# Pooling and attention gates of a decoder layer's merge: four of eight K pairs by seven products instead of eight

## The reference

```python
g_pool, g_attn, g_ret = split(sigmoid(u @ w_gate), 3)      # w_gate: 2048 x 6144
merged = g_pool * (pool_out @ w_pool_out) + g_attn * (attn_out @ w_attn_out) \
       + g_ret * (ret_out @ w_ret_out)                     # K = 1024, 1024, 2048
return merged @ w_out
```

## Time and profile before

| | us |
|---|---|
| median of 3 runs (2372.71 to 2373.50) | 2372.98 |
| the profiled execution | 2372.41 |
| its span, first to last instruction | 2370.6 |
| TensorE busy | 2356.8 (99%) |
| VectorE busy | 1750.5 (74%) |
| ScalarE busy | 1243.2 (52%) |

### The profile page before, as it was taken

How to read it: one execution, slowest core, us unless ns; L and a number is a source line. 1 busy time by engine, 2 the same in 40 slices (tenths; PEclk the granted TensorE clock), 3 DMA queues, 4 the chain that set the end, 5 groups by cost and what they waited for, 6 DMA issues and landing times. The chain is left out here.

```text
span 2370.6 us, 33710 instructions
## 1 busy us (share of the span) xinstructions
PE 2356.8 (99%) x10613; PEld 1945.0 (82%) x10613; DVE 1750.5 (74%) x2057; ACT 1243.2 (52%) x1490; POOL 205.9 (9%) x398
## 2 busy tenths in 40 slices
PE   9999999999999999999999999999999999999998
PEld 7888888888888888888888888888888888888887
DVE  6999999978876555655545545555799999997886
ACT  6555555555545454444544444444655555555553
POOL 1212112110000000000000000000021211211000
PEclk9999999999999999999999999999999999999999
DMA  7766666665675555565656566655666666666665
GB/s 236 220 212 203 216 219 222 212 221 191 209 240 172 163 175 178 159 188 157 204 187 196 190 198 193 189 185 194 207 213 227 206 218 207 221 212 214 204 204 195
DMA packets 266605, 477.44 MB, mean 201 GB/s; under 512 B 21152, under 2 KB 54608, under 8 KB 265392
## 3 DMA queue, kind: packets, MB, share of 16 engines
q1 hardware_dynamic: 252752, 453.04, 59.6%
q0 software_dynamic: 13616, 23.53, 3.0%
q10 hardware_dynamic: 176, 0.07, 0.0%
HBM read 460.84 MB, written 4.19 MB: 196 GB/s over the span
## 5 line engine op out<-in xcount | busy, mean ns | idle before, releaser
L1260 ACT ACTIVATE w_hi<-w_raw 128x1024 fp32r<-128x1024 f32 (+1 forms) x848 | 863.6, 1021 | 985.9 <-PE acc L781 732.1
L1641 DVE TENSOR_TENSOR w_lo<-w_raw,w_hi 128x1024 fp32r<-128x1024 f32 (+1 forms) x848 | 991.8, 1172 | 507.5 <-ACT w_hi L1260 503.0
L779 PE MATMUL acc<-w_hi,xT_hi 128*128 128x512 f32 x1552 | 609.2, 393 | 1.0 <-DVE w_lo L1641 1.0
L781 PE MATMUL acc<-w_hi,xT_lo 128*128 128x512 f32 x1552 | 604.4, 389 | 0.0
L780 PE MATMUL acc<-w_lo,xT_hi 128*128 128x512 f32 x1552 | 604.1, 389 | 0.0
L779 PEld LDWEIGHTS acc<-w_hi,xT_hi 128*128 128x128 f32 x1552 | 291.4, 188 | 63.0 <-issue 2.5
L781 PEld LDWEIGHTS acc<-w_hi,xT_lo 128*128 128x128 f32 x1552 | 291.3, 188 | 61.1
L780 PEld LDWEIGHTS acc<-w_lo,xT_hi 128*128 128x128 f32 x1552 | 291.5, 188 | 59.3
L696 POOL DMA_DIRECT2D act_raw<-blocks x352 | 174.9, 497 | 736.4 <-DVE blocks L1978 647.5
L779 PE MATMUL acc<-w_hi,act_hi 128*128 128x512 f32 x560 | 218.2, 390 | 0.1
L780 PE MATMUL acc<-w_lo,act_hi 128*128 128x512 f32 x560 | 217.9, 389 | 0.0
(11 more groups left out here) (269 smaller groups left out, 2601.4 us busy)
## 6 DMA issues: line engine op xcount, KB each, us to landing
w_raw<-in_ffn_up_dram SPq DMA_DIRECT2D x352, 512.0 KB, 4.2
w_raw<-in_ffn_down_dram SPq DMA_DIRECT2D x176, 512.0 KB, 4.2
w_raw<-in_w_gate_dram SPq DMA_DIRECT2D x96, 512.0 KB, 3.8
w_raw<-in_w_in_dram SPq DMA_DIRECT2D x72, 512.0 KB, 3.6
w_raw<-in_w_in_dram SPq DMA_DIRECT2D x128, 256.0 KB, 2.9
w_raw<-in_w_ret_out_dram SPq DMA_DIRECT2D x32, 512.0 KB, 3.7
w_raw<-in_w_out_dram SPq DMA_DIRECT2D x32, 512.0 KB, 4.2
act_raw<-blocks POOLq DMA_DIRECT2D x352, 32.0 KB, 3.8
```

What stands on the lines that cost most here:

```text
L779: pe.matmul(pair[m][:, :], xh, wh, start=(first and kk == 0), stop=False)
L781: mm = pe.matmul(pair[m][:, :], xl, wh, start=False, stop=(last and kk == KG - 1))
L1260: act.activation(w_hi[:, s, cols], w_raw[:, s, cols], ACT.Copy).then_inc(w_rounded, 1)
L1641: dve.tensor_tensor(w_lo[:, s, cols], w_raw[:, s, cols], w_hi[:, s, cols].bitcast(f32), ALU.subtract).then_inc(w_split, 1)
```

## The change

- The merge's order of strips becomes: retention gate (groups 0 to 7), retention branch (8 to 15), pool gate and attention gate together (16 to 31), pool branch (32 to 35), attention branch (36 to 39).
- In the joint stretch, K pairs 4 to 7 of both gates are quads at groups (17, 18), (21, 22), (24, 25), (28, 29); K pairs 0 to 3 are plain. `merge_products` does the seven products with four extra banks; VectorE makes the weight sums, VectorE and ScalarE split them, and VectorE combines the banks into `gate_sb` and `hid_sb`, on which ScalarE then does the sigmoids.
- The weight sums use `dt_raw`, `dt_hi`, `dt_lo`. So h is stored to the output tensor behind the first block's residual (`h_away(0)`) and loaded again behind the last quad of the merge (`h_again`); the load of `post_gain` moves from the last head to the same place, ahead of it.
- Once, in pass 0: the ratio of the norm factors is spread over the columns by one matmul of ones with a diagonal (behind group 1), VectorE scales tile 1 with it and makes the token sums at steps 2 to 8.

Left out of the diff below: the allocation of semaphores, the quad counters, the token sums (one product and four sums of 128 x 512 and 128 x 1024), and `h_parked` and `h_back` counts.

```diff
+MERGE_QUADS = ((17, 18, 4), (21, 22, 5), (24, 25, 6), (28, 29, 7))
+MERGE_GATE0 = {16: 0, 19: 1, 20: 2, 23: 3}
+MERGE_GATE1 = {26: 0, 27: 1, 30: 2, 31: 3}
+NMQ = len(MERGE_QUADS)
+M_KT = KG * MERGE_QUADS[0][2]
+M_TILES = KG * NMQ
+M_JOINT, M_POOL, M_ATT = 2 * GD, 4 * GD, 4 * GD + GH
+NM = 4 * GD + 2 * GH
...
+        MQ_A = {ng: j for j, (ng, nu, k) in enumerate(MERGE_QUADS)}
+        MQ_B = {nu: j for j, (ng, nu, k) in enumerate(MERGE_QUADS)}
+        MT_AT = {ng - 3 + pair: (j, pair) for j, (ng, nu, k) in enumerate(MERGE_QUADS) for pair in range(2)}
...
+                for n in range(NM):
+                    for quads in (MQ_A, MQ_B):
+                        if n - SLOTS in quads:
+                            sp.wait_ge(t_summed, 3 * (merge_quad(c, quads[n - SLOTS]) + 1))
+                            sp.sem_inc(slot_summed, 1)
+                    w, col = source[n]
+                    cols = w[:, :, ds(c * STRIP + col, STRIP)]
+                    if n == GD:
+                        sp.wait_ge(w_split, group("merge", c, n) + 1)
+                        sp.sem_inc(slot_split, 1)
+                        sp.dma_start(slot(n % SLOTS), cols).then_inc(w_landed[n % SLOTS], 16)
+                    else:
+                        load("merge", c, n, cols)
...
+            def h_away(blk):
+                for m in range(MT):
+                    wait_h(pool, blk, m, CH - 1)
+                    pool.dma_start(out[0][m * P:(m + 1) * P, :], h[:, m, :]).then_inc(h_parked, 16)
+            def h_again(last_quad, src):
+                pool.wait_ge(t_used, last_quad + 3)
                 for m in range(MT):
                     pool.dma_start(h[:, m, :], src[m * P:(m + 1) * P, :]).then_inc(h_back[m], 16)
...
-            wait_filled(pool, "o", 3, KVH - 1)
-            wait_read(pool, "inner", 0, KVH - 1)
+            wait_strip_read(pool, "merge", CH - 1, 3)
             pool.dma_start(post_gain[:, :], on_all(t["mix_post"][0], D)).then_inc(gain_landed, 16)
+            h_again(merge_quad(CH - 1, NMQ - 1), out[0])
             residual(1)
-            for m in range(MT):
-                wait_h(pool, 1, m, CH - 1)
-                pool.dma_start(out[0][m * P:(m + 1) * P, :], h[:, m, :]).then_inc(h_parked, 16)
+            h_away(1)
...
+            def merge_products(c, j):
+                ng, nu, k = MERGE_QUADS[j]
+                first, last = j == 0, j == NMQ - 1
+                gate0, gate1 = acc[pair_of("merge", 2)], acc[pair_of("merge", 3)]
+                def x(kk, m):
+                    rows = slice(m * P, (m + 1) * P)
+                    return xT_hi[:, KG * k + kk, rows], xT_lo[:, KG * k + kk, rows]
+                def w(n, kk):
+                    cols = slice(kk * STRIP, (kk + 1) * STRIP)
+                    return w_hi[:, n % SLOTS, cols], w_lo[:, n % SLOTS, cols]
+                def s(y):
+                    return mx_hi[:, y, j, :], mx_lo[:, y, j, :]
+                def tt(y):
+                    return dt_hi[:, y, :], dt_lo[:, y, :]
+                if first:
+                    for b in range(4):
+                        claim("m", b, c)
+                pe.wait_ge(w_split, group("merge", c, ng) + 1 + SLOTS)
+                p1 = three(bank[0][:, :], *x(0, 0), *w(ng, 0), first, last)
+                if last:
+                    p1.then_inc(filled[0], 1)
+                three(gate0[0][:, :], *x(1, 0), *w(ng, 1), False, last).then_inc(w_used, 1)
+                if first:
+                    pe.wait_ge(acc_read[pair_of("merge", 3)], strip_in_pair("merge", c, 3) + 1)
+                pe.wait_ge(w_split, group("merge", c, nu) + 1 + SLOTS)
+                pe.wait_ge(mx_split, 1)
+                three(gate1[0][:, :], *s(3), *w(nu, 1), first, False).then_inc(w_used, 1)
+                pe.wait_ge(t_split, 2 * merge_quad(c, j) + 1)
+                p7 = three(bank[3][:, :], *s(2), *tt(1), first, last)
+                p5 = three(bank[1][:, :], *s(0), *tt(0), first, last)
+                pe.wait_ge(t_split, 2 * merge_quad(c, j) + 2)
+                p6 = three(bank[2][:, :], *s(1), *tt(2), first, last)
+                if last:
+                    p7.then_inc(filled[3], 1)
+                    p5.then_inc(filled[1], 1)
+                    p6.then_inc(filled[2], 1)
+                three(gate0[1][:, :], *x(1, 1), *tt(3), False, last).then_inc(t_used, 1)
+            def second_gate(c, n):
+                s, k = n % SLOTS, KG * MERGE_GATE1[n]
+                pe.wait_ge(w_split, group("merge", c, n) + 1 + SLOTS)
+                for kk in range(KG):
+                    for m in range(MT):
+                        rows, cols = slice(m * P, (m + 1) * P), slice(kk * STRIP, (kk + 1) * STRIP)
+                        mm = three(acc[pair_of("merge", 3)][m][:, :], xT_hi[:, k + kk, rows], xT_lo[:, k + kk, rows],
+                                   w_hi[:, s, cols], w_lo[:, s, cols], m == 1 and n == min(MERGE_GATE1) and kk == 0,
+                                   n == max(MERGE_GATE1) and kk == KG - 1)
+                mm.then_inc(w_used, 1)
...
+                for n in range(GD):
+                    products("merge", c, n, xT_hi, xT_lo, KG * n, 0, n == 0, n == GD - 1)
+                    if n == 1:
+                        with pe.If(c < 1):
+                            pe.wait_ge(ratio_ready, 1)
+                            claim("ratio", 2)
+                            pe.matmul(bank[2][:, 0:P], ones[:, :], ratio_diag[:, :], start=True, stop=True).then_inc(filled[2], 1)
+                    if n == 3:
+                        with pe.If(c < 1):
+                            ret_transposes(KVH - 1)
+                for b in range(2):
+                    wait_read(pe, "ret", b, KVH - 1)
+                for k in range(GD):
+                    products("merge", c, GD + k, *branch[2], KG * k, 1, k == 0, k == GD - 1)
+                for n in range(M_JOINT, M_POOL):
+                    if n in MERGE_GATE0:
+                        products("merge", c, n, xT_hi, xT_lo, KG * MERGE_GATE0[n], 2, n == min(MERGE_GATE0), False)
+                    if n in MQ_B:
+                        merge_products(c, MQ_B[n])
+                    if n in MERGE_GATE1:
+                        second_gate(c, n)
+                wait_read(pe, "pool", 1, KVH - 1)
+                for k in range(GH):
+                    products("merge", c, M_POOL + k, *branch[0], KG * k, 4, k == 0, k == GH - 1)
+                wait_read(pe, "pv0", 1, KVH - 1)
+                def product(n, tiles=range(MT)):
+                    k = n - M_ATT
+                    products("merge", c, n, *branch[1], KG * k, 5, k == 0, k == GH - 1, tiles)
+                tail(product, NM, c, CH - 1, transpose_merged)
...
+                    if n == 6:
+                        with act.If(c < 1):
+                            act.wait_ge(mx_summed, 1)
+                            act.activation(mx_hi[:, :, :, :].rearrange("p a b n -> p (a b n)"),
+                                           mx_raw[:, :, :, :].rearrange("p a b n -> p (a b n)"), ACT.Copy).then_inc(mx_rounded, 1)
+                    if n in MT_AT:
+                        j, pair = MT_AT[n]
+                        both = slice(2 * pair, 2 * pair + 2)
+                        act.wait_ge(t_summed, 3 * merge_quad(c, j) + 2 * pair + 1)
+                        act.activation(dt_hi[:, both, :], dt_raw[:, both, :], ACT.Copy).then_inc(t_rounded, 1)
+                    if n == GD - 1:
                         wait_strip(act, "merge", c, n)
-                        if k:
-                            wait_strip_read(act, "merge", c, 2 * k - 1)
-                        pair = pair_of("merge", 2 * k)
                         for m in range(MT):
-                            last = act.activation(gate_sb[:, m, :], acc[pair][m][:, :], ACT.Sigmoid,
+                            last = act.activation(gate_sb[:, m, :], acc[pair_of("merge", 0)][m][:, :], ACT.Sigmoid,
                                                   scale=rs_pre[:, 1, m:m + 1])
-                        last.then_inc(acc_read[pair], 1)
+                        last.then_inc(acc_read[pair_of("merge", 0)], 1)
+                    if n == MERGE_QUADS[-1][0]:
+                        wait_filled(act, "m", 0, c)
+                        wait_strip_read(act, "merge", c, 1)
+                        act.activation(gate_sb[:, 0, :], bank[0][:, :], ACT.Copy).then_inc(read[0], 1)
+                    for gate, k in ((gate_sb, 2), (hid_sb, 3)):
+                        if n == M_POOL + k - 4:
+                            wait_strip_read(act, "merge", c, k)
+                            for m in range(MT):
+                                last = act.activation(gate[:, m, :], gate[:, m, :], ACT.Sigmoid, scale=rs_pre[:, 1, m:m + 1])
+                            last.then_inc(gates_done, 1)
...
+            rs = rs_pre[:, 1, :]
+            link(dve.reciprocal(inv_rs[:, :], rs))
```

(86 more changed lines are left out.)

131 lines of the change are left out of this document (78 added, 53 removed).

## The result

| | before | after |
|---|---|---|
| median of 20 runs each, us | 2372.84 | 2376.50 |
| lowest to highest | 2372.30 to 2374.77 | 2375.66 to 2378.48 |
| ratio of the two | | 1.0015, 95% interval 1.0009 to 1.0022 |
| span of the profiled execution | 2370.6 | 2374.8 |
| TensorE busy, VectorE busy | 2356.8, 1750.5 | 2352.4, 1842.0 |

The changed kernel is 3.7 us slower, 0.15%: inside the 0.2% that I called no change, 0.9 us above the forecast of 2375.6. The interval leaves 1 out, so the small loss is real. The 48 matmuls are gone, and TensorE waits for a little more than they were worth.

A forecast was written before the change was run, and what follows sets the result against it. TensorE bounds the kernel: matmuls times a pitch of 0.2267 us, plus waits. Terms -10.9 + 7.8 + 4.0 + 1.7 = +2.6 us on the median 2372.98 gave 2375.6 us, range 2367 to 2382.

The forecast's parts named there:

- What is removed: Four quads in each of four merge passes take 21 matmuls instead of 24: 48 fewer, 10.9 us gained.
- The quad three groups after another: Third quad, groups 24 and 25: TensorE waits for w_lo and dt_lo, 1.95 us a pass, 7.8 us in all.
- The first quad's accumulator: First quad of each pass waits until VectorE has read retention's strip: 1.0 us a pass, 4.0 us in all.
- The ratio: Once, behind group 1 of the first pass: stall 1.4 us plus matmul 0.3, 1.7 us (bounds 1 and 2.5).
- The end of the stretch: VectorE frees pair 0's accumulator before group 32, 0.7 us to spare: nothing, up to 4 x 0.5 us if landings are slower.
- the token sums: VectorE's sums in groups 2 to 8 of the first pass: nothing, at worst 2 us.
- the moved parts: Retention first, h stored and reloaded, post_gain loaded in the last pass: nothing, apart from the memory burst rival.
- The two waits that repeat: In each of four passes, third quad's wait of 1.95 us and first quad's accumulator wait of 1.0 us.
- the waits would be covered: Rival: TensorE does not stall at the quads after all, 2363.8 us; chance 0.1.
- only one of the two waits shows: Rival: without the accumulator's wait 2371.6 us, or with the three-group wait halved 2371.7; chance 0.15.
- The memory burst: Rival: last pass, groups 32 to 39, 3.15 MB delay weight loads by 4.6 us; 2380.2, up to 2384; chance 0.2.
- its point of decision: In the memory burst rival, a weight load makes TensorE late once its landing takes above 8.4 us.

The follow-up runs named there:

- e5: Changed kernel with ratio matmul behind group 2, gated first at step 15, quad's low part before its sums, second dt_lo before ordinary low part; 2363.35 us.
- e6: Changed kernel with the second quad at groups (20, 21) instead of (21, 22), so distances are 3, 4, 4; 2376.24 us.
- e7: Changed kernel with retention's accumulator read first and quads at (16, 17), (20, 21), (24, 25), (28, 29), all distances four; 2367.89 us.
- e3: Changed kernel with VectorE making the low part of a quad's first group before sum13; 2372.60 us.
- e2: Changed kernel with VectorE reading retention's accumulator (gated) at the head of step 15; 2372.70 us.
- e8: Kernel before with only the moved parts: retention first, h parked, post_gain and h loaded in the last pass; no quads, no ratio; 2372.98 us.
- e10: Changed kernel with one 128x512 copy on VectorE ahead of gated at step 15, to lengthen TensorE's wait; 2377.83 us.
- e4: Changed kernel with a quad's low part before sum13 and the second dt_lo before the ordinary group's low part; 2376.11 us.
- e9: e4's kernel with one 128x512 copy on VectorE ahead of gated at step 15, to lengthen TensorE's wait; 2377.61 us.

## Why the prediction was right

- **What is removed.** 48 matmuls at 0.2267 us, 10.9 us: e5, which has nearly nothing but this left, is 9.9 us below its kernel before (2373.25 to 2363.35), and its merge 9.5 us shorter (436.94 against 446.42). Of the 1.4 us between, 4 x 0.2 are dt_lo and 0.1 the ratio matmul; 0.5 are in pieces too small to place.
- **The quad three groups after another.** Predicted 1.95 us a pass, in three pieces, by w_lo once and by dt_lo twice; measured 2.13, in these pieces. e6 moves it with the distance, e7 removes it with the distance, e3 shortens it by shortening the chain. The missing 0.2 us are the slow restarts behind each piece, of which I had counted one, and a fourth piece of 0.07 us at group 24, which I had called just in time.
- **The first quad's accumulator.** Predicted 1.0 us a pass, measured 1.09; e2 removes it.
- **The ratio.** Predicted 1.7 us (1.4 wait, 0.3 matmul), measured 1.2 (1.1 and 0.1). In proportion this term is the furthest off. The memset and the product ended 0.24 us after the memset's start, where I had put 0.5; the four linked instructions started 0.2 us apart, a little more than the 0.16 to 0.17 of the estimate. VectorE wrote the ratio at 1144.99 and not after 1144.8 + 0.1, and this merge began 0.6 us later than the one before, so the ratio was 0.4 to 0.5 us sooner on the same clock.
- **The end of the stretch, the token sums, the moved parts.** Predicted nothing, and no wait of TensorE stands there in the profile after; e8 shows the moved parts alone at nothing. (The landing of group 33 in that sum should read 9.49 and not 9.45 us, 641.14 less 631.65; nothing hangs on it.)
- **The sum.** -10.9 + 4.4 + 8.5 + 1.2 = +3.2 us, where the merge of the profile grew by 3.35 and the medians differ by 3.7; the forecast was +2.6. The two waits that repeat were set 1.1 us too low and the ratio 0.5 us too high, so part of the closeness is luck: the errors cancel by half.
- **The runs that lie higher.** Three of the 20 runs lie a microsecond or two above the others. They were not profiled, but e10's profiled execution was such a one, 1.8 us above its median, with no drop behind its waits. It is 1.4 us late already at its first matmul of the merge (1140.05 against 1138.63), and lost it in the first 12 us of the program, where matmuls start 0.43 us apart, the pace of e4's drops, for a little longer than in the changed kernel:

```profile
10.34 0.63 PE L842 MATMUL acc<-w_lo,xT_hi 128*128 128x512 f32 x1
10.77 0.63 PE L843 MATMUL acc<-w_hi,xT_lo 128*128 128x512 f32 x1
```

In the changed kernel's profile these two start at 9.37 and 9.60. The profiled executions of e2 and e7 are 1.2 to 1.5 us late at the same place. The column of the granted clock shows 1.00 there, so that it was the clock is not shown.
- **The rivals.** The list of TensorE's waits refutes that the waits would be covered, and e5 shows what it would have been worth; it refutes too that only one of the two waits shows. The memory burst took place and did no harm. But its point of decision was wrong: loads landed after 9.0 us in the median, above my 8.4, and ScalarE waited 6.0 us for one, with TensorE busy all through. This is the burst's stretch, by the columns of e4's:

```profile
1565.00:1570.00 5.00, 5.00 (x24) 4.14 (x23) 2.73 (x3) 1.80 (x2) 0.00 (x0) 1.00 0.97 388
```

The DMA issues from 1558 to 1580 us (KB of each, median us to landing):

```profile
w_raw<-in_w_out_dram SPq DMA_DIRECT2D x6, 512.0 KB, 9.0
```

And ScalarE's wait in its timeline:

```profile
1574.45 1.06 ACT L1382 ACTIVATE w_hi<-w_raw 128x1024 fp32r<-128x1024 f32 x1 [5.99 <-DMA w_raw<-in_w_out_dram]
```

The late loads were those of the next section's first groups, which TensorE wants only behind the tail's eight half groups. I had taken the run-ahead of a plain stretch for it. What was left for the first of these groups stands in the trace: VectorE made its low part from 1575.55 to 1576.77 (the row joins it with the next group's), and TensorE began the section's first matmul 3.0 us later.

```profile
1575.55 2.50 DVE L1778 TENSOR_TENSOR w_lo<-w_raw,w_hi 128x1024 fp32r<-128x1024 f32 x2 [1.29 <-ACT w_hi L1382]
...
1579.78 0.47 PE L841 MATMUL acc<-w_hi,xT_hi 128*128 128x512 f32 x1
```

## What to carry to other kernels

When an operation that saves matmuls is copied from one stretch to another, copy the distances too: one set of sums that just covers four groups cost 2.1 us at three in the same order of work. Lay the two timelines side by side from the rows of the stretch where it already works, shift one of them by the difference, and read off who is late; here that gave the two waits that repeat to 0.2 us a pass, while the one that rested on estimates was off by 0.5. Then look at the order on the late engine before its load: three swaps on VectorE and one matmul moved a group later turned a loss of 0.15% into a gain of 0.4%, with the same instructions on every engine.

## What the runs showed of the hardware

- Two waits of 1.89 us in one execution: behind one of them eight matmuls ran at a granted clock of 0.50, behind the other none (e4). The drop added 1.6 us to the idle 1.89.
- A wait costs more than its idle time in the trace: 1.09 us for 0.85, and 2.13 for 1.07 in three pieces. Behind each of these waits in pass 0 the next matmul came 0.31 to 0.34 us later and not 0.23.
- A copy of 128x512 float32 on VectorE from SBUF to SBUF took 0.42 us (e9) and one from an accumulator bank 0.68 us (before). I had reckoned with the latter. The Trainium skill ("VectorE: DVE Perf Modes", section "Mode 2×_2P — use both read ports for one tensor") gives an operation with one source in SBUF both read ports, which one with a source in PSUM can't have; the trace agrees with the direction.

```profile
1188.63 0.42 DVE L2471 COPY m_u<-gate_sb 128x512 f32<-128x512 f32 x1
```
